# Block 1 of a fp32 two-block kernel with its tokens held in the order of their remainder by four

## The reference

```
# block 1, twice (l = 0, 1)
h = rms_norm(x, g_mix[l]);  proj = h @ w_in[l]            # a | b | c | gates
y_a = mla_mixer(...)            # attention over low ranks, 8 heads, all 512 keys
y_b = dilated_mixer(q_b, k_b, v_b)
      # 4 heads x 3 patterns: dilation 1, 4, 16, a band of 64, 64, 64 on either side within
      # the tokens of one remainder; the patterns mixed by a softmax over their log-sums
y_c = neighbourhood_mixer(q_c, k_c, v_c, rpb)
      # tokens as a grid of 8 rows x 64 columns, 8 heads, 8 x 16 keys around each token, a bias
x = x + (gate_a * (y_a @ w_pa) + gate_b * (y_b @ w_pb) + gate_c * (y_c @ w_pc)) @ w_o
x = x + (silu(h2 @ w1) * (h2 @ w3)) @ w2                  # h2 = rms_norm(x, g_ffn[l])
# then x = rms_norm(x, g_final)
# block 2: retention (causal, with decay over the distance of tokens) and SwiGLU,
#          then a gated linear recurrence over the tokens and SwiGLU
```

## Time and profile before

| | |
|---|---|
| median of 3 runs | 3415.31 us (3414.6 to 3418.52) |
| the profiled execution's own time | 3414.56 us |
| its span in the profile | 3412.8 us |
| granted PE clock over the span | 0.993 |
| busy: PE, PEld, DVE, ACT, POOL | 98%, 81%, 53%, 39%, 18% |
| mean HBM traffic, DMA share in q1 | 87 GB/s, 26.1% |
| chain that ended last | PE 85%, DVE 7%, ACT 4%, issue 2%, POOL 2% |
| PE in this chain by line | L309 (matmuls) 84% |

### The profile page before, as it was taken

The page is one execution under the profiler, slowest core; times in us unless marked ns, Lnnn a source line. Parts: engine busy times, 40 slices in busy tenths (PEclk is TensorE's granted clock), DMA queues, the critical chain, the costliest instruction groups (busy, mean ns, idle before and its releaser), DMA issues.

```text
span 3412.8 us, 38569 instructions
## 1 busy us (share of the span) xinstructions
PE 3349.6 (98%) x15644; PEld 2780.6 (81%) x15644; DVE 1793.6 (53%) x2674; ACT 1317.7 (39%) x2018; POOL 601.4 (18%) x518
## 2 busy tenths in 40 slices
PE   8999999999999999999999999999999999999998
PEld 7788778888888877878888888888888888788887
DVE  6755564544427654665444355553544248864433
ACT  4643453323226533543322333332333238743321
POOL 1421122011003320221110012210211024531101
PEclk9999999999999999999999999999999999999999
DMA  4012223222221111322222322222222312223332
GB/s 135 32 63 74 76 92 105 96 99 99 93 99 61 52 62 50 106 92 99 93 99 99 103 82 84 84 85 89 87 94 95 102 63 97 87 75 96 95 102 84
DMA packets 85425, 296.92 MB, mean 87 GB/s; under 512 B 9472, under 2 KB 11776, under 8 KB 85248
## 3 DMA queue, kind: packets, MB, share of 16 engines
q1 hardware_dynamic: 85248, 294.47, 26.1%
HBM read 292.33 MB, written 2.10 MB: 86 GB/s over the span
## 4 chain that ended last, share of the span: by engine, by line
PE 85%; DVE 7%; ACT 4%; issue 2%; POOL 2%; DMA 0%; SPq 0%; POOLq 0%; DVEq 0%; ACTq 0%
PE bank L309 84%; PE bank L312 2%; DVE wl L553 1%; ACT wh L526 1%; POOL u_g L573 1%; DVE small L1214 1%; DVE u_uc L549 1%; POOL u_q L573 0%; DVE u_h L3084 0%; ACT c_k L526 0%; DVE m_ptl L553 0%; ACT b_v L526 0%; DVE m_qf L543 0%; ACT m_p L529 0%; POOL x L573 0%
## 5 line engine op out<-in xcount | busy, mean ns | idle before, releaser
L553 DVE TENSOR_TENSOR wl<-raw,wh 128x1024 fp32r<-128x1024 f32 (+1 forms) x532 | 686.6, 1294 | 870.9 <-ACT wh L526 867.8
L309 PE MATMUL bank<-zh,wh 128*128 128x512 f32 (+1 forms) x2668 | 1040.4, 390 | 11.5 <-ACT zh L526 7.2
L309 PE MATMUL bank<-zl,wh 128*128 128x512 f32 (+1 forms) x2668 | 1028.5, 385 | 5.4 <-DVE zl L556 5.3
L309 PE MATMUL bank<-zh,wl 128*128 128x512 f32 (+1 forms) x2668 | 1028.7, 386 | 3.1 <-DVE wl L553 3.1
L526 ACT ACTIVATE wh<-raw 128x1024 fp32r<-128x1024 f32 (+1 forms) x532 | 557.6, 1052 | 563.8 <-PE bank L309 510.0
L309 PEld LDWEIGHTS bank<-zh,wh 128*128 128x128 f32 x2668 | 505.1, 189 | 114.7 <-ACT zh L526 7.5
L309 PEld LDWEIGHTS bank<-zh,wl 128*128 128x128 f32 x2668 | 504.7, 189 | 107.8 <-DVE wl L553 6.8
L309 PEld LDWEIGHTS bank<-zl,wh 128*128 128x128 f32 x2668 | 505.1, 189 | 103.0 <-DVE zl L556 7.4
L309 PE MATMUL bank<-f_mh,wh 128*128 128x512 f32 (+1 forms) x748 | 284.7, 381 | 0.0
L309 PE MATMUL bank<-f_mh,wl 128*128 128x512 f32 (+1 forms) x748 | 282.8, 378 | 0.0
L309 PE MATMUL bank<-f_ml,wh 128*128 128x512 f32 (+1 forms) x748 | 281.7, 377 | 0.0
(11 more groups left out here) (340 smaller groups left out, 4610.0 us busy)
## 6 DMA issues: line engine op xcount, KB each, us to landing
raw<-in_wts SPq DMA_DIRECT2D x530, 512.0 KB, 3.3
c_nb<-in_c_bias SPq DMA_DIRECT2D x16, 384.0 KB, 3.1
x<-in_xT SPq DMA_DIRECT2D x8, 256.0 KB, 6.4
out<-x SPq DMA_DIRECT2D x16, 128.0 KB, 1.8
b_mask<-in_b_mask SPq DMA_DIRECT2D x2, 576.0 KB, 3.8
r_d<-in_decay SPq DMA_DIRECT2D x4, 256.0 KB, 2.7
raw<-in_wts SPq DMA_DIRECT2D x2, 256.0 KB, 3.2
m_t<-in_mla_tab SPq DMA_DIRECT2D x2, 256.0 KB, 5.1
```

Source lines behind the costliest of these rows:

```text
L309: return self.e.matmul(out, l, r, start=start, stop=stop, skip_group_check=inside)
L553: return self.e.tensor_tensor(out, src, b32(hi), ALU.subtract)
```

## The change

The tokens of block 1 are held by remainder from the input on: place 128 q + i holds token 4 i + q. The host puts x and the two rotary tables of block 1 in this order; masks, biases and weights are the same. Every PE operand that had stride 4 in block 1 is now a contiguous piece of 128 columns. `rrow` is copied as it stands, and the result of the dilated branch is written as it stands.

The neighbourhood branch turns between remainder order (place = 128 q + 16 r + c/4) and grid order (8 c + r) with access patterns of four dimensions; the grid side has a stride of 32 elements (128 bytes) where it had 8.

The last residual of block 1 turns the tokens back: it reads `x[j]` and the bank as they are and writes into another tile, `x2[j]`, with a stride of 4 elements. `x2` is one new tile and then x[0] to x[6], so tile j overwrites x[j-1], and each of these eight instructions waits for the one before it. Block 2 works on `x2`.

No instruction of any engine is added, taken out or put in another place; only their access patterns differ, and the seven waits of the residual are new.

```diff
-def cr(ap):
-    return ap.rearrange("p (r c) -> p r c", r=8)
-def rc(ap):
-    return ap.rearrange("p (c r) -> p r c", r=8)
-def perm4(ap):
-    return ap.rearrange("p (i r) -> p r i", r=4)
+TOKENS = "p (q r c) -> p q r c", dict(q=4, r=8)
+GRID = "p (c q r) -> p q r c", dict(q=4, r=8)
+def by_token(ap):
+    return ap.rearrange(TOKENS[0], **TOKENS[1])
+def by_grid(ap):
+    return ap.rearrange(GRID[0], **GRID[1])
...
+        self.x2 = [T("x2", 59)] + self.x[:7]
...
-        cut = (lambda ap, t: ap[:, t::4]) if strided else (lambda ap, t: ap[:, 128 * t:128 * t + 128])
-        return lambda k, t: cut(self.m.zh[k], t), lambda k, t: cut(self.m.zl[k], t)
+    def z_tokens(self):
+        return lambda k, t: part(self.m.zh[k], t, 128), lambda k, t: part(self.m.zl[k], t, 128)
...
+def x_of(m, N):
+    return m.x2 if N[0] == "ret" else m.x
...
-def scalar_rows(L, N, strided):
-    m = L.m
+def scalar_rows(L, N):
     L.wait_ge("st", "rows", *N)
-    out, src = m.rrow, m.bank[7]
-    if strided:
-        out, src = out.rearrange("p (i r) -> p r i", r=4), src.rearrange("p (r i) -> p r i", r=4)
-    L.cp(out, src).then_inc(*L.tell("rr", *N))
+    L.cp(L.m.rrow, L.m.bank[7]).then_inc(*L.tell("rr", *N))
...
 def vector_shifted(L, f, ps):
-    r = cr(L.m.rrow)
-    L.tt(rc(f[:, 64:512]), cr(ps)[:, :, 0:56], r[:, :, 0:56], ALU.mult)
-    return L.tt(rc(f[:, 0:64]), cr(ps)[:, :, 56:64], r[:, :, 56:64], ALU.mult)
+    p, r = by_token(ps), by_token(L.m.rrow)
+    L.tt(by_grid(f[:, 64:512]), p[:, :, :, 0:14], r[:, :, :, 0:14], ALU.mult)
+    return L.tt(by_grid(f[:, 0:64]), p[:, :, :, 14:16], r[:, :, :, 14:16], ALU.mult)
...
-            L.mm(sa, m.b_q0[hh][:, r::4], perm4(m.b_k0[hh]), True, False)
-            L.mm(sa, m.b_q0[hh][rw, r::4], perm4(m.b_k0l[rw]), False, True).then_inc(*L.tell("qk", *key, i, 0))
+            L.mm(sa, part(m.b_q0[hh], r, 128), m.b_k0[hh], True, False)
+            L.mm(sa, part(m.b_q0[hh][rw], r, 128), m.b_k0l[rw], False, True).then_inc(*L.tell("qk", *key, i, 0))
...
-            L.mm(sb[:, 0:128], qk[2][rw, r::4], qk[3][rw, r::4], True, True)
-            L.mm(sb[:, 128:256], qk[4][rw, r::4], qk[5][rw, r::4], False, True, True).then_inc(*L.tell("qk", *key, i, 1))
+            q1, k1, q2, k2 = [part(x[rw], r, 128) for x in m.b_qk[p][2:]]
+            L.mm(sb[:, 0:128], q1, k1, True, True)
+            L.mm(sb[:, 128:256], q2, k2, False, True, True).then_inc(*L.tell("qk", *key, i, 1))
...
-            vector_y_add(L, m.b_yt, m.b_yf, i // 10, *key, view=YV[0], oview=YV[1])
+            vector_y_add(L, m.b_yt, m.b_yf, i // 10, *key)
...
-    L.stt(rc(m.c_qf), cr(m.bank[c_bank(p, 0)]), -0.125, cr(m.rrow), ALU.mult, ALU.mult).then_inc(*L.tell("ev", "c", l, p, 0))
+    L.stt(by_grid(m.c_qf), by_token(m.bank[c_bank(p, 0)]), -0.125, by_token(m.rrow), ALU.mult, ALU.mult).then_inc(
+        *L.tell("ev", "c", l, p, 0))
...
-            vector_y_add(L, m.b_yt, m.b_yf, (it - 5) // 2, *key, view=NV[0], oview=NV[1])
+            vector_y_add(L, m.b_yt, m.b_yf, (it - 5) // 2, *key, view=GRID, oview=TOKENS)
...
-            L.tt(m.x[j], m.x[j], m.bank[bank(j)], ALU.add).then_inc(*L.tell("xx", *N, j))
+            x, ps, o = m.x[j], m.bank[bank(j)], x_of(m, N)[j]
+            if N[0] == "ret":
+                x, ps, o = [ap.rearrange("p (q i) -> p q i", q=4) for ap in (x, ps)] + [
+                    o.rearrange("p (i q) -> p q i", q=4)]
+                if j:
+                    L.wait_ge("xx", *N, j - 1)
+            L.tt(o, x, ps, ALU.add).then_inc(*L.tell("xx", *N, j))
...
+def in_remainders(a):
+    return np.ascontiguousarray(np.concatenate([a[..., q::4] for q in range(4)], axis=-1))
...
+    mla, bt = in_remainders(mla), in_remainders(bt)
...
-    d["xT"] = np.ascontiguousarray(a["x"][0].T.reshape(8, 128, S).transpose(1, 0, 2).reshape(128, 8 * S))
+    d["xT"] = np.ascontiguousarray(in_remainders(a["x"][0].T).reshape(8, 128, S).transpose(1, 0, 2).reshape(128, 8 * S))
```

More of the change, by code:

```diff
@@ L461, in tiles_of, with sums @@
         return hi, lambda k: part(ap[1], k)
-    def sums(self, ps, strided, at, src, start):
-        cut = (lambda r: src[:, r::4]) if strided else (lambda r: src[:, 128 * r:128 * r + 128])
+    def sums(self, ps, at, src, start):
         for r in range(4):
             first = start and r == 0
-            i = self.mm(ps[:, at + r:at + r + 1], cut(r), self.m.ones, first, first or r == 3, not first)
+            i = self.mm(ps[:, at + r:at + r + 1], part(src, r, 128), self.m.ones, first, first or r == 3, not first)
         return i
@@ L474, in rows, with stat @@
         return i
-    def stat(self, N, strided):
+    def stat(self, N):
         def go():
@@ L481, in go @@
             self.wait_ge("ev", "ones")
-            self.sums(ps, strided, 0, self.m.sqa, True).then_inc(*self.tell("st", "stat", *N))
+            self.sums(ps, 0, self.m.sqa, True).then_inc(*self.tell("st", "stat", *N))
         return go
@@ L599, in weights @@
             self.inside = False
+def x_of(m, N):
+    return m.x2 if N[0] == "ret" else m.x
 def scalar_x(L, N, i, g, also=None):
     m = L.m
-    L.cp(m.zh[i], m.x[i], g[:, i:i + 1]).then_inc(*L.tell("zh", *N, i))
+    x = x_of(m, N)[i]
+    L.cp(m.zh[i], x, g[:, i:i + 1]).then_inc(*L.tell("zh", *N, i))
     if i > 1:
         L.wait_ge("sq", *N, i - 1)
-    L.fn(m.sqt if i else m.sqa, m.x[i], ACT.Square).then_inc(*L.tell("cp", "sq", *N, i))
+    L.fn(m.sqt if i else m.sqa, x, ACT.Square).then_inc(*L.tell("cp", "sq", *N, i))
     if also is not None:
@@ L614, in scalar_x @@
             L.wait_ge("sq", "b", *N, i - 1)
-        L.fn(m.sp if i else m.sqb, m.x[i], ACT.Square, scale=also[:, i:i + 1]).then_inc(*L.tell("cp", "sqb", *N, i))
+        L.fn(m.sp if i else m.sqb, x, ACT.Square, scale=also[:, i:i + 1]).then_inc(*L.tell("cp", "sqb", *N, i))
 def vector_x(L, N, i, g, also=False):
@@ L621, in vector_x @@
     L.wait_ge("zh", *N, i)
-    L.lo_scaled(m.zl[i], m.x[i], g[:, i:i + 1], m.zh[i]).then_inc(*L.tell("zl", *N, i))
+    L.lo_scaled(m.zl[i], x_of(m, N)[i], g[:, i:i + 1], m.zh[i]).then_inc(*L.tell("zl", *N, i))
     if i:
@@ L730, in tensor_bv @@
     keys = [("bv", l, p, r) for r in range(4)]
-    L.turned(keys, 3, 8, L.z_tokens(True), bv_desc(l, p), BV_BANK[p], [("lo",) + n for n in keys], extra)
+    L.turned(keys, 3, 8, L.z_tokens(), bv_desc(l, p), BV_BANK[p], [("lo",) + n for n in keys], extra)
 def scalar_bv(L, l, p, rs=range(4)):
@@ L811, in tensor_mix @@
     b = [("b", l, 0, 0, w) for w in range(2)]
-    L.group(b, 8, L.z_whole(), b_desc, (4, 5), [("cp",) + n for n in b], {1: L.stat(N, True), 4: L.spread(N)})
+    L.group(b, 8, L.z_whole(), b_desc, (4, 5), [("cp",) + n for n in b], {1: L.stat(N), 4: L.spread(N)})
     def squares():
@@ L817, in squares @@
         L.wait_ge("cp", "sqq", l, 2)
-        L.sums(ps, False, 0, m.sqa, True)
-        L.sums(ps, False, 4, m.sqkv, False).then_inc(*L.tell("st", "q", l))
+        L.sums(ps, 0, m.sqa, True)
+        L.sums(ps, 4, m.sqkv, False).then_inc(*L.tell("st", "q", l))
     def rows():
@@ L2051, in tensor_ffn1 @@
     quad = [F + (w, i) for i in range(2) for w in range(2)]
-    L.group(quad, 8, L.z(*N), w13_desc, range(4), [("ev",) + n for n in quad], {3: L.stat(N, False), 5: L.spread(N)})
+    L.group(quad, 8, L.z(*N), w13_desc, range(4), [("ev",) + n for n in quad], {3: L.stat(N), 5: L.spread(N)})
     for i in range(2, FF):
@@ L2194, in squares @@
         L.wait_ge("sq", "b", "ret", 0, 7)
-        L.sums(ps, False, 0, m.sqa, True)
-        L.sums(ps, False, 4, m.sqb, False).then_inc(*L.tell("st", "stat", "ret"))
+        L.sums(ps, 0, m.sqa, True)
+        L.sums(ps, 4, m.sqb, False).then_inc(*L.tell("st", "stat", "ret"))
     def rows():
@@ L2254, in tensor_ret @@
         keys = [("rv", h, t) for t in range(4)]
-        L.turned(keys, 4, 8, L.z_tokens(False), ret_wide(2048, h), [far(h) + t for t in range(4)],
+        L.turned(keys, 4, 8, L.z_tokens(), ret_wide(2048, h), [far(h) + t for t in range(4)],
                  [("lo",) + n for n in keys], {4 + kt: scores(h, kt) for kt in range(4)})
         keys = [("rgate", h, t) for t in range(4)]
-        L.turned(keys, 4, 8, L.z_tokens(False), ret_wide(4096, h), [near(h) + (2, 3, 0, 1)[t] for t in range(4)],
+        L.turned(keys, 4, 8, L.z_tokens(), ret_wide(4096, h), [near(h) + (2, 3, 0, 1)[t] for t in range(4)],
                  [("ev",) + n for n in keys], {k: values(h, qt) for qt, k in enumerate((2, 3, 5, 7))})
@@ L2655, in scalar_post @@
                 L.wait_ge(*x_ready(s, n, h, False))
-                L.cp(half(m.zh[n], h), half(m.x[n], h), g[:, n:n + 1]).then_inc(*L.tell("zh", "z2", s, n, h))
-                L.fn(half(m.mb[n], h), half(m.x[n], h), ACT.Square).then_inc(*L.tell("cp", "xsq", s, n, h))
+                L.cp(half(m.zh[n], h), half(m.x2[n], h), g[:, n:n + 1]).then_inc(*L.tell("zh", "z2", s, n, h))
+                L.fn(half(m.mb[n], h), half(m.x2[n], h), ACT.Square).then_inc(*L.tell("cp", "xsq", s, n, h))
             if h == 0 and n == POST_AT[s]:
```

(6 more changed lines are left out.)

18 lines of the change are left out of this document (7 added, 11 removed).

## The result

| | before | changed |
|---|---|---|
| median of 4 runs | 3416.91 us (3414.6 to 3418.52) | 3371.97 us (3367.59 to 3374.92) |
| ratio | | 0.9868 (95% interval 0.9851 to 0.9885) |
| profiled execution, own time and span | 3414.56, 3412.8 us | 3367.59, 3365.8 us |

The change takes 45 us off; forecast were 3367 us and a range from 3347 to 3390. The median lies 5 us over the forecast.

The account below looks back on a forecast made before the run. PE, busy 98% of 3412.8 us, was taken as the bound. Kept gains of 26 us a layer, 52 in all, less 4 for clock, took 3414.56 to 3366.6, a median of 3367 us (range 3347 to 3390).

Parts of the forecast that it names:

- the rival that all of it is kept: Whole kernel: DVE and ACT keep up, so all 70 us of PE's gain stay, 3345 us; chance 0.13.
- the one of a first pass at DVE's pace: Dilated units 1 to 7 keep little because DVE sets the pace: 3385 to 3394 us, partly 3378; chance 0.18.
- the scores of a unit: Dilated unit, first score to second fill matmul: 2.76 us falls to about 1.3, saving 1.47; 47 us over 32 units.
- second pass: Dilated branch, 8 units: 2.1 us of slack at POOL exceeds the 1.47 at stake, all kept, 11.8 us a layer.
- the first pass: Dilated units 1 to 7: six keep 1.47 us, one with a late DVE weight split none; 8.8 us a layer.
- Mix stage: First projections with first tensor_bv as fill: PE soon waits for DVE, 1.3 us a layer kept of 5.8.
- Unit 0: Second tensor_bv and first dilated unit: chain-bound at POOL, 4.1 us a layer kept of 7.3 at stake.
- Long strides cost nothing: DVE forms with 128 bytes of stride, 20 a layer: cost taken as 0, range up to 12 us.
- The rival of slower than before: Neighbourhood branch: strided DVE forms at 4.3 us each or more bind it; about 3415 to 3451 us; chance 0.03.
- that of long strides: DVE's strided forms: 12 us more DVE work reach PE nearly whole, 3378 to 3385 us; chance 0.10.
- The last residual: End of block 1: eight strided operations, 1.1 us instead of 0.68; about 1 us of delay hidden by 6 us cover.
- the separate 4 us for the clock: Two mix stages and two units 0: new PE waits lose clock, 1 us each, 4 in all (0 to 13).

Follow-up runs that it names:

- e3: Changed kernel with the score products that took 64 partitions (b_k0l, b_qk) taking all 128: 3361.82 us, ratio 0.9842 to the kernel before.
- e1: Changed kernel with only the stationary operand of the four tensor_bv calls (the values) strided by 4 again: 3380.77 us, ratio 0.9893 to the kernel before.
- e2: Changed kernel with only the operands of the dilated score products strided by 4 again: 3406.28 us, ratio 0.9970 to the kernel before.
- e7: The changed kernel run again unedited, its second profiled execution: 3371.54 us, ratio 0.9872 to the kernel before.
- e5: Changed kernel with the values' banks reordered and a weight split moved behind unit 0's mask in the first pass: 3372.58 us, ratio 0.9872 to the kernel before.

## Why the prediction was right

**The direction and the size** followed from PE's share and from the slack at each handover, and both held for the whole: PE's own work fell by 58 us (3349.6 to 3291.4 busy us on the page) where the prediction had 70, and some 45 reached the end. So the rival that all of it is kept fell, and so did the one of a first pass at DVE's pace.

**The step that was mis-sized is the scores of a unit.** The contiguous sum was put at 1.3 us and the gain at 1.47; measured were 1.62 and 1.14. The 0.1 for each 128-column product, the 0.23 for each 512-column one and the 0.3 for the first fill matmul, the prediction's first after a change of operands (204.78 to 205.11 in the earlier trace rows), were right, as e3 shows with 0.11, 0.23 and 0.32. Missing was a term: the load that isn't drawn ahead where the number of partitions changes, 0.2 us at each of the two changes of a unit. Over the units behind unit 0 the forecast was 41 us, measured are 32, and 42.5 in e3.

**The slack was read rightly.** In the second pass every unit keeps what PE gains (0.87 to 1.19 us). In the first pass six of the seven units of layer 0 do (1.08 to 1.20, and 1.42 to 1.60 in e3, so the slack would have borne the forecast's 1.47 too), and the one with the late weight split gains 0.08, as the earlier trace rows had said. In layer 1 this unit gained 0.98, which the prediction had put at nothing.

**Mix stage: wrong in each layer, and right in sum by luck.** 1.3 us each were forecast, and -0.2 and 2.8 measured; the second execution has -2.6 and 1.8, a sum of -0.8. In layer 0 all of it became a wait for m_zkvl, with a clock of 0.71 behind it. The stretches of the trace after, in the columns of the earlier trace rows:

```profile
60.00:65.00 5.00, 1.50 (x8) 1.18 (x7) 4.97 (x8) 1.94 (x3) 0.00 (x0) 0.95 0.33 105
65.00:70.00 5.00, 5.00 (x20) 4.54 (x20) 3.15 (x5) 2.66 (x4) 0.00 (x0) 0.71 0.00 0
```

PE is busy 1.5 of 5 us while DVE has 4.97, and then PE's clock is down for part of the next 5. `rrow` gave its half microsecond, 0.60 us (timeline of ACT) where the earlier trace rows had 1.10:

```profile
40.52 0.60 ACT L527 ACTIVATE rrow<-bank 128x512 f32<-128x512 f32 x1 [7.08 <-PE bank L315]
```

**Unit 0** kept 3.1 and 4.1 us where 4.1 was forecast. e1 shows that it is tensor_bv that pays here. Unit 0's own 1.14 is waited away: e2, without it, kept 3.0 and 4.5 between the same marks, as much as the changed kernel (3.1 and 4.1, 3.2 and 4.5 in e7). The wait is not quite the one forecast: in the first trace after PE waits for b_v from DVE ahead of the fill (2.41 and 1.33 us), and not for POOL ahead of the transposes, where e1 waits 0.99 in both layers and e7 1.01 in layer 1. e5 showed that an order of banks doesn't get it back.

**Long strides cost nothing,** the value that was taken. The forms with 128 bytes of stride are a little shorter than they were with 32: the c_qf form (first before, then after) and the b_yf sums, whose row before is in the earlier trace rows (last view: the tile, ns min, median, max). The b_yf sums with a minimum of 662 ns are those of the dilated branch, contiguous now:

```profile
L549 DVE SCALAR_TENSOR_TENSOR c_qf<-bank,rrow 128x512 f32<-128x512 f32 x8 | 9.0, 1127 | 0.2 <-PE bank L309 0.2
```

```profile
L550 DVE SCALAR_TENSOR_TENSOR c_qf<-bank,rrow 128x512 f32<-128x512 f32 x8 | 8.7, 1088 | 0.6 <-PE bank L312 0.6
```

```profile
L544 DVE TENSOR_TENSOR b_yf<-bank,b_yt x24: 662/1082/1108, 235.6 to 1458.7; 64x512 f32<-64x512 f32 x24
```

The rival of slower than before, and that of long strides, fall with these lines. The Trainium skill, page "Advanced Engine Details and Errata", section "Memory Cachelines", has it that an access pays when each element falls into a new line of 16 bytes; with 1082 ns at 128 bytes, where 1048 to 1184 ns stood at 16 and 32, the trace now agrees for a stride far beyond a line too.

**The last residual** costs 2.26 us for two tiles, which were 1.38, and is hidden as forecast: the last sum of squares ends at 1934.18 and PE asks for it at 1939.70 (timeline of DVE, before and after, then of PE).

```profile
1972.93 1.38 DVE L543 TENSOR_TENSOR x<-x,bank 128x512 f32<-128x512 f32 x2 [1.12 <-PE bank L309]
```

```profile
1928.28 2.26 DVE L544 TENSOR_TENSOR x<-x,bank 128x512 f32<-128x512 f32 x2 [1.12 <-PE bank L312]
...
1933.49 0.69 DVE L544 TENSOR_TENSOR sqb<-sqb,sp_tmp 128x512 f32<-128x512 f32 x1
```

```profile
1939.70 0.95 PE L312 MATMUL bank<-small,sqa 128*128 128x1 f32 x8
```

**Two errors nearly cancelled.** The units gave 9 us less than forecast. In the profiled execution 5 us came back in the neighbourhood branch and block 2, where none was forecast, and the mix stage and unit 0, with their loss of clock in them, gave 9.9 us, 0.9 less than the 10.8 forecast without it, so that of the separate 4 us for the clock only about 1 was spent. In the second execution, without such luck, these two places gave 6.9 us, 3.9 less than the 10.8: there the 4 us were spent, and the gain of 39.4 lies under the forecast's 48 by the 9 of the units alone. The medians say 43 to 45, so part of the nearness to 48 is luck.

## What to carry to other kernels

Put data once into the order in which the engine that bounds the kernel reads it, and let an engine with time to spare do the turning: a strided PE operand cost 0.06 us in each 384-column matmul and over 1 us in each set of scores, while DVE's turning cost the same at 16, 32 and 128 bytes of stride. Then go through the handovers one by one: a gain on PE is kept where the slack is larger than the gain (second pass), and becomes a wait where it is smaller (mix stage); moving one operation of DVE forward only helps if nothing behind it is due. And count the places where the number of partitions of the stationary operand changes, since a load isn't hidden there.

## What the runs showed of the hardware that was not expected

- A weight load with another number of partitions (64 after 128, or 128 after 64) starts only when its matmul could start: 0.34 us between starts where equal forms have 0.23, and 10 us over the units of both layers (e3). It holds for every such place of the trace after: 64 loads from 128 to 64 and 62 back (those ahead of which PE waits left out) start at most 3 ns ahead of their matmul. Loads with 128 after 128 start 0.22 us ahead in the median, those with 64 after 64 0.11 us, so it is the change and not the 64.
- The granted clock differs between executions of one kernel at one and the same pair of waits (1.00 and 0.83 around 465 us; 0.68 to 1.00 in the nine traces), and two profiled executions of the changed kernel differ by 7.6 us, of which 0.5 us is the start of the first matmul. Differences of under 0.1% can't be seen in a median of four runs here; in the starts of the same matmuls they can, place by place.
